# Latents and rotary key as one product by tokens with 416 moving columns, and block 2's values with 512

## The reference, cut to what matters

```
z = h @ w_in[l]
q_lat, kv_lat, k_rope, mla_gate, conv_in, conv_gate = split(z)   # 512, 256, 64, 1024, 2048, 1024 columns
q  = rms_norm(q_lat,  q_lat_g[l])  @ w_q_up[l]      # 8 heads of 192
kv = rms_norm(kv_lat, kv_lat_g[l]) @ w_kv_up[l]     # 8 heads of 128 + 128
# heads' norms, rotary part, causal attention, times silu(mla_gate)
# conv_in: gated, a causal depthwise convolution with 31 taps, layer norm, silu, w_pw, times silu(conv_gate)
x = x + gate * (concat(mla_out, conv_out) @ w_out[l])
```

## Time and profile before

| | |
|---|---|
| three runs | 2579.53, 2583.24, 2583.43 us; median 2583.24 |
| span of the profiled execution | 2578.3 us |
| own time of the profiled execution | not given beside its span |
| PE busy | 2368.3 us (92%) |
| weight loads busy | 2236.9 us (87%) |
| DVE, ACT busy | 1773.9 us (69%), 909.5 us (35%) |
| mean granted clock of TensorE | 0.938 |
| read from HBM | 553.72 MB |

### The profile page before, as it was taken

One profiled execution on the slowest core, in us unless ns is written; L12 is line 12 of the kernel. 1 busy time (PEld: TensorE's weight loads), 2 busy tenths in 40 slices (PEclk: granted clock), 3 DMA queues, 4 the chain that ended last, 5 costly groups with the idle time before them and its releaser, 6 DMA issues.

```text
span 2578.3 us, 41885 instructions
## 1 busy us (share of the span) xinstructions
PE 2368.3 (92%) x16533; PEld 2236.9 (87%) x16533; DVE 1773.9 (69%) x2368; ACT 909.5 (35%) x1330; POOL 41.3 (2%) x57
## 2 busy tenths in 40 slices
PE   2289999899899998998998999988999999999998
PEld 2189998779899987798997999768999999999998
DVE  6777798776777988668959583577876656654443
ACT  1053322323543223234333341135544444433333
POOL 0000000000000000005000000000000000000000
PEclk7588899899988999999999998989999999999999
DMA  8869654776596647677968794236865555555552
GB/s 302 316 213 333 237 172 145 247 231 226 198 333 241 183 141 255 204 246 225 348 203 274 255 363 149 74 123 200 273 219 182 184 179 184 182 165 184 180 184 94
DMA packets 413234, 557.41 MB, mean 216 GB/s; under 512 B 25139, under 2 KB 362103, under 8 KB 412868
## 3 DMA queue, kind: packets, MB, share of 16 engines
q1 hardware_dynamic: 409536, 550.70, 64.9%
q0 software_dynamic: 1120, 2.18, 0.5%
q10 hardware_dynamic: 2468, 3.07, 0.3%
HBM read 553.72 MB, written 2.17 MB: 216 GB/s over the span
## 4 chain that ended last, share of the span: by engine, by line
PE 79%; DVE 12%; DMA 4%; issue 2%; ACT 2%; DVEq 0%; ACTq 0%; SPq 0%
PE gemm L1346 70%; DVE ada_acc L913 4%; DMA ada_raw<-in_ada_w 3%; PE stat L1365 2%; PE stat L1373 1%; DVE w_lo L940 1%; DVE scr L968 1%; DVE h_lo L973 1%; PE bankS L1490 1%; PE bankO L1395 1%; PE bankS L1489 1%; ACT w_hi L667 1%; DVE ss L1111 1%; PE stat L1357 0%; ACT h_full L703 0%
## 5 line engine op out<-in xcount | busy, mean ns | idle before, releaser
L940 DVE TENSOR_TENSOR w_lo<-w_raw,w_hi 128x1024 fp32r<-128x1024 f32 (+1 forms) x564 | 669.7, 1198 | 441.3 <-ACT w_hi L667 439.0
L1346 PE MATMUL gemm<-h_hi,w_hi 128*128 128x256 f32 x3136 | 905.0, 289 | 45.5 <-DVE h_lo L973 19.9
L1346 PE MATMUL gemm<-h_lo,w_hi 128*128 128x256 f32 x3136 | 899.8, 287 | 0.0
L1346 PE MATMUL gemm<-h_hi,w_lo 128*128 128x256 f32 x3136 | 899.3, 287 | 0.0
L667 ACT ACTIVATE w_hi<-w_raw 128x1024 fp32r<-128x1024 f32 (+1 forms) x564 | 571.6, 1028 | 751.7 <-PE gemm L1346 631.1
L1346 PEld LDWEIGHTS gemm<-h_hi,w_hi 128*128 128x128 f32 x3136 | 615.9, 196 | 48.9 <-issue 33.7
L1346 PEld LDWEIGHTS gemm<-h_lo,w_hi 128*128 128x128 f32 x3136 | 615.6, 196 | 0.4
L1346 PEld LDWEIGHTS gemm<-h_hi,w_lo 128*128 128x128 f32 x3136 | 614.8, 196 | 0.0
L913 DVE SCALAR_TENSOR_TENSOR ada_acc<-ada_raw,c_act,ada_acc 128x1024 f32<-128x1024 f32 x360 | 460.1, 1295 | 33.0 <-DMA ada_raw<-in_ada_w 29.6
L1346 PE MATMUL gemm<-G_hi,w_hi 128*128 128x256 f32 x704 | 200.1, 284 | 3.1 <-DVE w_lo L940 3.1
L1346 PE MATMUL gemm<-G_lo,w_hi 128*128 128x256 f32 x704 | 199.9, 284 | 0.0
(11 more groups left out here) (267 smaller groups left out, 2613.3 us busy)
## 6 DMA issues: line engine op xcount, KB each, us to landing
w_raw<-in_w_in SPq DMA_DIRECT2D x264, 512.0 KB, 5.6
ada_raw<-in_ada_w SPq DMA_DIRECT2D x192, 512.0 KB, 5.3
w_raw<-in_w_up SPq DMA_DIRECT2D x176, 512.0 KB, 3.5
ada_raw<-in_w_ada SPq DMA_DIRECT2D x168, 512.0 KB, 5.2
w_raw<-in_w_out SPq DMA_DIRECT2D x96, 512.0 KB, 5.3
w_raw<-in_w_down SPq DMA_DIRECT2D x64, 512.0 KB, 3.6
ada_late<-in_w_ada SPq DMA_DIRECT2D x24, 512.0 KB, 4.3
w_raw<-in_w_down SPq DMA_DIRECT2D x32, 384.0 KB, 3.6
```

The costliest lines, as they stand in the source:

```text
L940: dve.tensor_tensor(w_lo[:, fixed % PARTS, 0:sz], w_raw[:, fixed % RAW, 0:sz], w_hi[:, fixed % PARTS, 0:sz].bitcast(F32), ALU.subtract).th ...
L1346: last = pe.matmul(half(g, k, q), left, right, start=(kt == 0 and j == 0), stop=(u == len(g.units) - 1 and t == nk - 1 and j == len(parts) ...
```

## The change

- `lat` and `krope` become one product of kind "b": two blocks of 416 columns (832 = 512 + 256 + 64), eight units of 2 tiles each (`wide`). 192 products in a layer. ACT copies the results to `lat_tok[token][column]`, and the last 64 columns to `krope` as well.
- The sums of squares are taken by ACT along the tokens' rows (`accum_out`), with the root; DVE takes four reciprocals and scales the rows. `lat_q` and `lat_kv` leave the `stat` bank's uses.
- Beside the units 1, 3 and 5 of `gate`, PE transposes two column tiles back (12 transposes in a layer), and ACT writes them to `lat` with the gain as scale.
- `vb` and `va` become two blocks of 512 columns, in eight units.
- A block may have more units than `PARTS`. `ahead` now prepares the follower's first four units beside the last block, and the rest of that first block (`part`) at the start of the follower's own `ahead`. This also holds for `down` (12 units), which was prepared in one piece after the last block of `upb`.

The core of the diff:

```diff
+LAT_STEPS = (1, 3, 5)
-        lat_sq = at("lat_sq", W1, [P, 6, T])
+        lat_sq = at("lat_sq", W1, [P, QLORA])
+        lat_tok = at("lat_tok", W1 + 8, [P, TT, QLORA + KVLORA + ROPE])
+        lat_ss = at("lat_ss", 118 + 736 / 1024, [P, 2, TT])
+        wide = [(k, UK // 2) for k in range(0, KT, UK // 2)]
+        LATB = O_GATE // 2
-            G["lat", l] = product("lat", wi, 3, CB, full, 3, "a", h_hi, h_lo, plain(0), ada=(2 + 3 * l, 0, 1))
-            G["krope", l] = product("krope", wi, 1, ROPE, full, 1, "b", h_hi, h_lo, plain(O_ROPE), ada=(2 + 3 * l, 12, 1))
+            G["lat", l] = product("lat", wi, 2, LATB, wide, 2, "b", h_hi, h_lo, lambda i, k, B: k * LATB,
+                                  ada=(2 + 3 * l, 0, 1))
-        G["vb"] = product("vb", w2, 4, CB, full, 2, "b", h_hi, h_lo, plain(O_QB + 2 * DC))
+        G["vb"] = product("vb", w2, 2, 2 * CB, wide, 2, "b", h_hi, h_lo, lambda i, k, B: O_QB + 2 * DC + k * 2 * CB)
-        G["va"] = product("va", w2, 4, CB, full, 2, "b", h_hi, h_lo, plain(O_VA), ada=(10, 0, 1))
+        G["va"] = product("va", w2, 2, 2 * CB, wide, 2, "b", h_hi, h_lo, lambda i, k, B: O_VA + k * 2 * CB, ada=(10, 0, 1))
...
-                elif follower is not None and len(follower.units) <= PARTS:
-                    prep(follower, 0, 0, (g, i, k), beside, done)
+                elif follower is not None:
+                    prep(follower, 0, 0, (g, i, k), beside, done, range(min(PARTS, len(follower.units))))
                 else:
                     done = None
                 if done is None:
                     finish(i, k)
-                if last and follower is not None and len(follower.units) > PARTS:
-                    prep(follower, 0, 0)
+            if len(g.units) > PARTS:
+                prep(g, 0, 0, part=range(PARTS, len(g.units)))
...
+                def lat_out(i, k, g=G["lat", l]):
+                    wait_full(act, g, i, k)
+                    for q in range(2):
+                        src = half(g, k, q)
+                        if k == 1:
+                            act.activation(krope[:, q, :], src[:, LATB - ROPE:LATB], ACT.Copy)
+                        freed(act.activation(lat_tok[:, q, k * LATB:(k + 1) * LATB], src, ACT.Copy), g, k)
+                ahead(act, G["lat", l], prep, lat_out)
                 wait_out(act, G["lat", l])
-                act.activation(lat_sq[:], lat[:], ACT.Square).then_inc(lat_squared, 1)
+                for s, (c0, c1) in enumerate(((0, QLORA), (QLORA, QLORA + KVLORA))):
+                    for t in range(TT):
+                        link(act.activation(lat_sq[:, 0:c1 - c0], lat_tok[:, t, c0:c1], ACT.Square,
+                                            accum_out=lat_ss[:, s, t:t + 1]))
+                    act.activation(lat_ss[:, s, :], lat_ss[:, s, :], ACT.Sqrt, scale=1.0 / (c1 - c0),
+                                   bias=eps_t[:]).then_inc(lat_std, 1)
...
-                dve.wait_ge(stat_read, USE[f"lat_kv{l}"] + 1)
-                link(dve.reciprocal(rstd[:], rstd[:]))
-                for j in range(6):
-                    ins = dve.scalar_tensor_tensor(out=lat[:, j, :], in0=lat[:, j, :], scalar=par[:, p0 + 64 + j:p0 + 65 + j],
-                                                   in1=rstd[:, 0 if j < 4 else 1, :], op0=ALU.mult, op1=ALU.mult)
-                ins.then_inc(lat_ready, 1)
+                dve.wait_ge(lat_std, 2 * l + 2)
+                link(dve.reciprocal(lat_ss[:], lat_ss[:]))
+                for s, (c0, c1) in enumerate(((0, QLORA), (QLORA, QLORA + KVLORA))):
+                    for t in range(TT):
+                        ins = dve.tensor_scalar(lat_tok[:, t, c0:c1], lat_tok[:, t, c0:c1], lat_ss[:, s, t:t + 1], None,
+                                                ALU.mult)
+                ins.then_inc(lat_scaled, 1)
...
-                pe.wait_ge(lat_squared, l + 1)
-                summed(f"lat_q{l}", [lat_sq[:, j, :] for j in range(4)])
-                summed(f"lat_kv{l}", [lat_sq[:, j, :] for j in (4, 5)])
                 multiply(G["ub", l])
-                multiply(G["gate", l])
+                def lat_turn(_, n, l=l):
+                    if n in LAT_STEPS:
+                        b = LAT_STEPS.index(n)
+                        pe.wait_ge(lat_scaled, l + 1)
+                        dst = tr_bank(LAT_TR[l] + b)
+                        for j in range(2):
+                            for t in range(TT):
+                                c = (2 * b + j) * P
+                                last = pe.transpose(dst[:, j * T + t * P:j * T + (t + 1) * P], lat_tok[:, t, c:c + P], ident[:])
+                        last.then_inc(tr_ready, 1)
+                multiply(G["gate", l], lat_turn)
```

More of the change, by code:

```diff
@@ L502, in ada_load, with load @@
                 sp.dma_start((ada_late if n == 11 and fixed >= LATE else ada_raw)[:, slot:slot + 1, :], src).then_inc(ada_loaded[slot], 16)
-            def load(g, i, k, before=None, _=None, __=None):
+            def load(g, i, k, before=None, _=None, __=None, part=None):
                 if g is G["upa"] and before[0] is not g:
                     sp.wait_ge(hA_ready, NHA)
-                for u, (k0, nk) in enumerate(g.units):
+                part = part or range(len(g.units))
+                for u in part:
+                    k0, nk = g.units[u]
                     n, fixed = g.unit(i, k, u)
@@ L515, in load @@
                     sp.dma_start(dst, src).then_inc(w_loaded[fixed % RAW], 16)
-                    for m, j, row, f, _ in ada_pieces(before, u, len(g.units)):
+                    for m, j, row, f, _ in ada_pieces(before, u, len(part)):
                         sp.wait_ge(ada_used, j + (AU * m - ASLOTS + 1))
@@ L524, in _ @@
                     ada_load(n, j // 2, j)
-            load(prods[0], 0, 0)
+            load(prods[0], 0, 0, part=range(PARTS))
             for g in prods:
@@ L654, in _, with prep @@
             act.activation(cosT[:], wrap[:, 1], ACT.Sin).then_inc(rope_done, 1)
-            def prep(g, i, k, before=None, beside=None, done=None):
-                for u, (k0, nk) in enumerate(g.units):
+            def prep(g, i, k, before=None, beside=None, done=None, part=None):
+                part = part or range(len(g.units))
+                for u in part:
+                    k0, nk = g.units[u]
                     n, fixed = g.unit(i, k, u)
-                    if done is not None and u == len(g.units) - 1 > 0:
+                    if done is not None and u == len(part) - 1 > 0:
                         done()
@@ L669, in prep @@
                     if beside is not None:
-                        for v in units_beside(before, u, len(g.units)):
+                        for v in units_beside(before, u, len(part)):
                             beside(before[1], v)
-                if done is not None and len(g.units) == 1:
+                if done is not None and len(part) == 1:
                     done()
@@ L737, in split_hi @@
                 act.activation(hi, src, ACT.Copy).then_inc(mix_hi_done, 1)
-            prep(prods[0], 0, 0)
+            prep(prods[0], 0, 0, part=range(PARTS))
             for l in range(LAYERS):
@@ L941, in prep @@
                                           w_hi[:, fixed % PARTS, 0:sz].bitcast(F32), ALU.subtract).then_inc(w_split, 1)
-                    for piece in ada_pieces(before, u, len(g.units)):
+                    for piece in ada_pieces(before, u, len(part)):
                         ada_add(*piece)
                     if beside is not None:
-                        for v in units_beside(before, u, len(g.units)):
+                        for v in units_beside(before, u, len(part)):
                             beside(before[1], v)
-                if done is not None and len(g.units) == 1:
+                if done is not None and len(part) == 1:
                     done()
```

37 lines of the change are left out of this document (19 added, 18 removed).

## The result

| | before | after |
|---|---|---|
| median of the runs | 2582.51 us (four, 2579.53 to 2583.43) | 2557.78 us (four, 2554.86 to 2559.85) |
| span of the profiled execution | 2578.3 us | 2558.1 us |
| mean granted clock | 0.938 | 0.941 |
| read from HBM | 553.72 MB | 553.72 MB |

The ratio is 0.9909, 95% interval [0.9892, 0.9927]: 24.7 us less, where 46 were forecast.

A forecast was written before the change was run, and what follows sets the result against it. PE's products were taken to bound the kernel, with short waits between. Savings of 12.7 + 14.1 + 13.4 - 2.6 + 7.3 + 1.4 = 46.3 us from the 2578.3 us span, plus 4.9, gave 2537 us; range 2519 to 2558.

The forecast's parts named there:

- stage of the latents, layer 0: Latents through ua: 75.8 us from 162.3 against 88.14, including a 2 us stall; 12.7 us saved.
- the same, layer 1: Latents' stage of layer 1, the same stretch against 89.57 us: 14.1 us saved.
- statistics, both: Reduction behind the latents' stage: 14.9 us become 8.2 as the sums of squares go; 6.7 us saved a layer.
- transposes: Twelve a layer on PE between units of the gate, 1.3 us each layer: 2.6 us lost.
- vb: Block 2's value product in 512-column records: 45.8 us become 41.5, less 0.3 us for the attention's wait.
- va: Block 2's other value product: 4.3 us saved by 512-column records, less 1 us for five sums at its end.
- down: First units split ahead of the last glu, so PE no longer waits for w_lo: 1.4 us saved.
- Nothing to add, and nothing to spare: Transfers in the latents' stage: 26.9 MB from 164.4 need 72 us at 375 GB/s, to 236, about when PE arrives.
- Transfers and DVE's burst bound the stage: Rival, chance 0.14: queue delays unit 20 and later by 8 us instead of 2, va's by 4; 2552 us.
- The record's price: Wide products: 176 ns per 416-column record and 216 per 512, load hidden; upper end 187 and 226.
- the reduction at about 239: Sign to look for in the trace: the reduction behind layer 0's latents' stage starts at about 239 us.
- The clock eats it: Rival, chance 0.13: unit 4's wait and the reduction each bring 17 us of half clock instead of 7; 2557 us.

The follow-up runs named there:

- half_bytes: Changed kernel, loading only half the columns of each modulation piece in groups 2 and 5, same instructions; 2542.5 us, ratio 0.9857.
- late_even_half: Changed kernel with ACT's copies into h_full later, modulation pieces spread evenly, and half the columns of pieces in groups 2 and 5 loaded; 2526.7 us, ratio 0.9810.
- late_full_before: Kernel before, with ACT's sixteen copies into h_full moved behind the first units of the latents' second block; 2568.9 us, ratio 0.9961.
- values_only: Kernel before, with only vb and va in blocks of 512 columns and the two-part preparation (down's too); 2574.7 us, ratio 0.9971.
- krope256: Kernel before, with 256 instead of 64 weight columns moving in the rotary key's product, 192 of them unused; 2567.2 us, ratio 0.9957.
- late_full_after: Changed kernel, with ACT's sixteen copies into h_full moved behind the w_hi of the latents' units 4 to 7; 2547.5 us, ratio 0.9884.
- even_after: Changed kernel, with the modulation's pieces spread evenly over the units of the latents and va; 2544.8 us, ratio 0.9867.
- late_even: Changed kernel with both the later copies into h_full and the evenly spread modulation pieces; 2532.0 us, ratio 0.9836.

## Why the prediction was off, step by step

| term | predicted | in the two traces |
|---|---|---|
| stage of the latents, layer 0 | 12.7 | 5.9 |
| the same, layer 1 | 14.1 | 6.6 |
| statistics, both | 13.4 | 13.5, less 2.8 of low clock behind |
| transposes | -2.6 | -2.6 |
| vb | 4.0 | 3.2 (2.7 over all kernels) |
| va | 3.3 | -2.6 (about 1 over all kernels) |
| down | 1.4 | 1.0 |
| not in the sum | | -1.9 |
| sum | 46.3 | 20.3 |

- **The step that failed** is "Nothing to add, and nothing to spare" for the transfers. The bytes were right: 26.9 MB were predicted, and 13, 313 and 376 GB/s over 8, 32 and 45.5 us are 27.2 MB, when the last load lands at 245.5. The start and the rate were wrong. The sum let a full queue run from 164.4 us; the loads of `w_raw` start again only when unit 4 is used (167.6), and are full from 200 on. So the queue was done at 245.5 and not at 236. TensorE waited 8.0 us ahead of the reduction, 4.4 more than the 3.6 of before, and 1.5 us elsewhere; half_bytes puts the cost of the transfers at 6.2 and 6.6 us, where the sum had a stall of 2 us a layer. The other 2.6 and 2.9 us missing in this stage are TensorE's own: wider records and low clock. The rival "Transfers and DVE's burst bound the stage" (0.14) is what happened in kind; half_bytes shows the transfers, and that the burst without them costs little. Its own numbers (8 us late in each layer in place of 2, va 4) were somewhat high for the stage and near for the sum.
- **The record's price** was the second. I took 176 and 216 ns, the columns alone, and kept 187 and 226 as the upper end: the upper end is what came, 189 and 227. Over 288 products of the latents and 384 of the values it is 3.7 and 4.2 us. The unsplit products have 2 to 3 ns above their columns (216 against 213, 322 against 320), and I took them as showing that a long record hides what it costs to load; split records carry 13 to 16 ns at 256, 416 and 512 columns. Under the transfers the latents' 1.9 us a layer hardly count; they are part of the 2.6 and 2.9 us above.
- **TensorE's part of the stage** was right otherwise. By the sum the stage of layer 0 should have taken 124.1 less 12.7, 111.4 us, and 109.4 without its stall. In late_even_half it takes 106.8 us with unit 4 about 4 us earlier, so 110.8 without that; the records' price is 1.8 us. The sign "the reduction at about 239" didn't follow from the sum: 162.3 + 75.8 + 3.6 is 241.7.
- **Statistics**: 6.7 us a layer between the reduction and ub, exactly. But I put the reduction with its low clock at 8.2 us, between 6.9 and 9.5, and it cost 9.7: half clock lasted until 261.4 us, 5.3 us into ub (2.7 lost), where before it lay to 270.9, 2.8 us into it (1.4 lost). With layer 1 (3.0 and 1.5 lost) that leaves 10.7 us in both layers.
- **Transposes**: three times 0.44 us beside the gate in each layer, as predicted by the row. The 275 ns of the Trainium skill ("TensorE: Matmul & The Clock Gate", Part 4; for bf16, float32 here) are not met; 110 ns are.
- **Clock**: unit 4 came at 163.0, with 10.2 us of half clock from 158.9 (6.8 in layer 1) where 7 were forecast. "The clock eats it" happened only at the reduction, with 17.1 and 13.7 us of half clock: in the stage and around the reduction together it was 27 us in layer 0 and 24 in layer 1, where that rival had 34.
- **down**: its first product is 2.0 us behind the last of up (2276.0 to 2278.05), 1.0 us saved.
- **What was not in the sum** (us gained or lost): qa -2.1 (17 us of half clock in place of 10.2); the stages from mLSTM to the MLP +3.7 (3.4 in place of 10.2); layer 1 from ub on -2.7 (6.8 us more of half clock between 981 and 1115); the start of layer 0 -0.6. By the list for qa above such stretches differ from one kernel's trace to the next; whether the change causes any of them is open.

Against the 46.3 us of the sum, the spans are 26.0 short: 14.3 in the latents' stage, 2.7 behind the statistics, 6.7 in the values, 0.4 in down, 1.9 outside of it. The medians differ by 4.5 us more than the two profiled spans, so the forecast's time was 21 us too low. Part of those 4.5 us is scatter: after, the profiled execution was the slowest of its four (2559.85 us, median 2557.78). How much of va's 2.6 us is va's is open: the stages spread by 6 us among kernels with the same va.

## What to carry to other kernels

Where a change makes TensorE faster in a stage with a DMA share near 1.0, sum the bytes from the moment at which the first new load can be issued, which is when a slot is given back, and not from the start of the stage; then look for what holds that moment up. Here two small reorderings on ACT and of the pieces were worth about as much together (19 to 26 us) as the change (25). And the price of a wider record is to be bounded from rows of the same kind: what the narrow one has above its columns stays until a row shows it gone.

## What the runs showed of the hardware

- A product with split weights took 0.120 us with 256 moving columns, 0.189 with 416 and 0.227 with 512, at a granted clock of 1.00. Columns at 2.4 GHz make 0.107, 0.173 and 0.213; the rest is 13 to 16 ns at these three widths. It isn't so for the thin product: 100 ns with 64 columns, which alone would be 27.
- Beside 96 products with 64 moving columns the clock fell to 0.50 for 17.1 us in both layers (13.7 to 20.5 in late_full_before and values_only); the same 96 with 256 columns didn't lower it, and the kernel was 11 us faster for four times the columns (krope256). The Trainium skill ("TensorE: Matmul & The Clock Gate", HAM oscillation) lays such falls to gaps in which TensorE waits for data; here PE shows as busy for 3.00 us of the 3.00 ahead of the fall and 15.00 of 15.00 in it, so the profile shows no such gap (the ends of products are modelled in it).
- At a DMA share of 1.04 to 1.07 the queue gave 369 to 385 GB/s over stretches of 32 and 36 us (after, late_full_after, even_after, late_even, krope256), and 352 where the modulation's pieces were half as large (half_bytes). Single loads of 512 KB then took 9.9 us in the chain where the median over the kernel is 5.4.
